# The norms of the first attention's queries and keys: roots and inverses by 32x32 blocks instead of whole tiles

## The chip, the cores and the metric

The kernel runs on one core of a Trainium2 chip. The metric is the device time of one execution in microseconds. A core has a matrix engine (TensorE, PE in the profile), a vector engine (VectorE, DVE), an engine for functions (ScalarE, ACT), a general engine (GpSimd, POOL) and a queue engine (SyncE, SP). Each executes its own instructions in the order in which they are written; semaphores order them against each other.

## The reference, cut to what matters

The model has two blocks on 512 tokens of 1024 features. The change lies in the attention of the first one: 16 query heads and 4 key heads of 64 features, each divided by the root of the mean of its squares, turned by the rotary tables, and then used in softmax attention.

```
q = rms_norm(q.reshape(b, s, N_Q_HEADS, HEAD_DIM), q_norm_w[l])
k = rms_norm(k.reshape(b, s, N_KV_HEADS, HEAD_DIM), k_norm_w[l])
v = v.reshape(b, s, N_KV_HEADS, HEAD_DIM)
q = axial_rope(q, cos_r, sin_r, cos_c, sin_c)
k = axial_rope(k, cos_r, sin_r, cos_c, sin_c)
attn = block_attention(q, k, v)
```

where rms_norm multiplies by `lax.rsqrt(jnp.mean(xf * xf, axis=-1, keepdims=True) + EPS)`.

## The kernel before, in words

Activations lie with features on the 128 partitions and the 512 tokens along them. A feature tile is 128 output features by 512 tokens: 24 matmuls on PE (8 blocks of the input, three products each, since every operand is split into a high and a low part), done by `feature_tile` (L1411), whose argument `mid` puts other PE work into the middle of the tile.

The weights come as one stream of slabs: SP loads them, ACT makes the high part (L775), POOL the low part (L716), and PE uses them. ACT's high parts are written out by `hi_upto` ahead of the tile at hand; POOL's other work (the rotation products L668 and L669 of a tile) stands at given slabs of this stream.

The list `QK` gives the order of the ten tiles of keys and queries: k0, q0, k1, q1, q2 up to q7. A tile holds two heads. After k1 come four value tiles (`value_tiles`, L1710), one for each 128 tokens, 24 half-width matmuls each. Key, query and value tiles use two PSUM banks in turn, so the fourth value tile needs the bank of the second one back.

For one tile the work is:
- ACT, `qk_copy` (L948): squares of the tile into `sq`, and a copy of the tile, with the norm's gain, into `t`; the copy frees the bank.
- DVE, `swap_halves` (L2440): a shuffle that swaps the halves for the rotation; POOL then makes its two products (`rotate`, L661).
- PE, `qk_stat` (L1491), in the middle of the next tile: `blk64` times the squares, into the bank `PST`. Each output row is the mean over the 64 features of its head, so all 64 rows of a head are equal. It waits for the semaphore `qk_std`, that is for the root of the tile before, as there is one `PST`.
- ACT, `qk_root` (L956): the root of 128x512 elements into `std`. It waits for PE's sum and for the inverse of the tile before. In ACT's order it stands ahead of the next tile's `qk_copy`; k1's root stands behind the copy of the first value tile and ahead of that of the second (L985 to L990); q5's stands ahead of the tanh of a gate tile, and q6's ahead of the row of maxima of head 0.
- DVE, `qk_inverse` (L2452): the reciprocal of 128x512 elements into `rstd`; then `rotated` (the add L2449, which waits for both of POOL's products) and the product with `rstd` (`turn_k` L2462, `turn_q` L2481), and for some tiles the split into high and low parts.

The last two tiles, q6 and q7, are inverted and turned inside the attention loop over 16 heads (L2543), their reciprocals in halves (`half_inverse`, L2457). In the same loop DVE takes the maxima of scores (`max_of`, L2520), which PE needs back before it writes the next scores of that kind; the four maxima of head 0 are taken between the shuffle and the inverse of q5 (L2532).

Of the kernel before, what the change touches and what calls it, by code (L numbers as in the profile page):

```python
# [9 lines left out]
ACT = mybir.ActivationFunctionType  # L10
# [3 lines left out]
P = 128  # L14
# [12 lines left out]
NCH = SEQ // P  # L27
# [241 lines left out]
for _name, _w in NORMS:  # L269
# [11 lines left out]
    _s += POOLED.get(_name, 0) == _w  # L281
    SUM_AT[_name] = _s
ADA_W = 2 * D_MODEL
ADA_G = 3
# [53 lines left out]
def build(nc, d):  # L338

    with ExitStack() as ctx:  # L340
# [64 lines left out]
        mx = [maxima[:, 0:NCH], maxima[:, NCH:2 * NCH]]  # L405
        inv_sum = small[:, 312:320]

        with Arena():
# [21 lines left out]
            with Arena():  # L430
# [7 lines left out]
                qF = sb("q_full", [P, QT, SEQ])  # L438
                std_last = sq_sum
            with Arena():  # L440
# [141 lines left out]
        chunks_added, sums_taken, sums_inverted, inverse_turned = exp_masked, st_done, rec_done, xt_done  # L582
        inverse_kept, q_high, inverse_spread = x_kept, e_ready, xs_sc
        ADDED_AT, SCANNED = 2 * PAIRS, PAIRS

        def token_half(half):
# [168 lines left out]
        def _(act):  # L755
# [200 lines left out]
            def qk_root(name):  # L956
                act.wait_ge(stat_mm, SUM_AT[name])
                if name == QK[-1]:
                    out = std_last
                else:  # L960
                    out = std
                    if QK_AT[name]:
                        act.wait_ge(qk_inv, QK_AT[name])
                A(out[:, :], PST[:, :], ACT.Sqrt, bias=eps).then_inc(qk_std, 1)

# [414 lines left out]
        def _(pe):  # L1380
# [110 lines left out]
            def qk_stat(name):  # L1491
                n = STAT_AT[name][0]
                pe.wait_ge(sq_ready, n + 1)
                if QK_AT[name]:
                    pe.wait_ge(qk_std, QK_AT[name])
                else:
                    pe.wait_ge(rows_kept, 1)
                mm(PST[:, :], blk64, sq[n % 2][:, :], start=True, stop=True).then_inc(stat_mm, 1)
# [262 lines left out]
            def take_sums(u, hh):  # L1761
# [3 lines left out]
                else:  # L1765
                    pe.wait_ge(qk_std, len(QK))
                for i in range(NCH):
# [358 lines left out]
        def _(ve):  # L2126
# [319 lines left out]
            def rotated(name):  # L2446
# [3 lines left out]
                v.settle()  # L2450

            def qk_inverse(name):  # L2452
                ve.wait_ge(qk_std, QK_AT[name] + 1)
                V.reciprocal(rstd[:, :], std[:, :]).then_inc(qk_inv, 1)  # L2454
                ve.wait_ge(qk_inv, QK_AT[name] + 1)

            def half_inverse(name, half):  # L2457
                ve.wait_ge(qk_std, QK_AT[name] + 1)
                src, w = std_last if name == QK[-1] else std, slice(half * SEQ // 2, (half + 1) * SEQ // 2)
                v(V.reciprocal(rstd[:, w], src[:, w]))  # L2460

            def turn_k(j):  # L2462
                swap_halves(("k", j))
                qk_inverse(("k", j))
                rotated(("k", j))
# [61 lines left out]
            for name in QK[:-2]:  # L2527
# [4 lines left out]
                if name == ("q", QT - 3):  # L2532
                    for i in range(NCH):
                        max_of(0, i)
                qk_inverse(name)
                turn_q(name[1])
# [3 lines left out]
                if name[1] == 1:  # L2540
                    split_q(2)
            swap_halves(QK[-2])
            for h in range(N_Q):  # L2543
                if h + 1 < N_Q:
                    for i in range(NCH):
                        max_of(h + 1, i)
                u = h // 2
                if h in (1, 3):
                    half_inverse(QK[-2], h // 2)
                if h == 5:  # L2550
                    turn_q(QT - 2)
                    swap_halves(QK[-1])
                if h in (7, 9):
                    half_inverse(QK[-1], h // 2 - 3)
                if h == 1:
# [682 lines left out]
```

## Time and profile before

| | |
|---|---|
| median of 3 runs | 1561.52 us (1560.51 to 1563.8) |
| the profiled execution | 1560.5 us, its span 1558.7 us |
| PE busy | 1528.3 us, 98% |
| DVE, ACT, POOL busy | 1139.1, 834.7, 907.3 us |
| granted clock of PE | 0.998 |
| the stage of key, value and query tiles | about 458 to 540 us of the span |
| the attention loop | about 540 to 650 us |

Busy time of an engine is the union of its instructions. Matmul ends are modelled, so for PE the distance from one matmul's start to the next says more than the busy share. Times in the rows are microseconds from the start of the span, and the time of one instruction in nanoseconds where a column says mean ns.

### The profile page before, as it was taken

How to read it: one execution, taken by the hardware profiler on the slowest of the kernel's cores; microseconds unless marked ns; L12 is line 12 of the kernel's file. 1: busy time of each engine (PE TensorE's matmuls, PEld its weight loads, DVE VectorE, ACT ScalarE, POOL GpSimd, SP SyncE). 2: the span in 40 equal slices, each digit the busy share in tenths (PEclk: the TensorE clock that was granted, in tenths of full speed). 3: DMA queues.
4: the chain of work that ended last, by engine and by line, in shares of the span. 5: the costliest groups of instructions: out<-in, count | busy, mean ns of one | idle time of the engine just before them, and what ended most of it. 6: DMA issues, size and time to landing. Idle time of an engine off the chain costs nothing.

```text
span 1558.7 us, 23051 instructions
## 1 busy us (share of the span) xinstructions
PE 1528.3 (98%) x7975; PEld 1235.0 (79%) x7975; DVE 1139.1 (73%) x1590; ACT 834.7 (54%) x1552; POOL 907.3 (58%) x644
## 2 busy tenths in 40 slices
PE   7999999999999999999999999999999999999998
PEld 4778888888878766687777888888888888888887
DVE  4799888888739888488459878877768895567542
ACT  4775765766633587423344444444458665454442
POOL 0556765766655876556846767776753467532314
PEclk9999999999999999999999999999999999999999
DMA  8434434434332300276622333333422334322212
GB/s 328 133 122 129 128 108 130 131 107 129 115 94 70 81 28 1 83 239 249 214 67 83 96 92 103 108 109 109 113 83 81 95 102 122 94 62 69 68 41 82
DMA packets 77485, 171.34 MB, mean 110 GB/s; under 512 B 8321, under 2 KB 10753, under 8 KB 73921
## 3 DMA queue, kind: packets, MB, share of 16 engines
q1 hardware_dynamic: 70064, 133.09, 28.7%
q10 hardware_dynamic: 7312, 36.83, 6.7%
q8 instruction: 65, 1.06, 0.3%
q14 instruction: 44, 0.35, 0.1%
HBM read 167.67 MB, written 2.23 MB: 109 GB/s over the span
## 4 chain that ended last, share of the span: by engine, by line
PE 64%; DVE 13%; issue 8%; POOL 6%; DMA 2%; ACT 2%; ACTq 0%; DVEq 0%; POOLq 0%; SPq 0%
PE bank L1401 8%; PE bank L1403 7%; PE bank L1402 7%; PE bank L1419 7%; PE bank L1422 7%; PE bank L1420 7%; POOL w_lo L716 6%; PE bank L1864 4%; DMA w_raw<-ws 2%; PE bank L1866 2%; DVE ada_acc L2155 2%; PE bank L1757 2%; DVE rstd L2454 2%; PE bank L2021 1%; PE bank L1695 1%
## 5 line engine op out<-in xcount | busy, mean ns | idle before, releaser
L716 POOL TENSOR_TENSOR w_lo<-w_raw,w_hi 128x512 fp32r<-128x512 f32 x440 | 644.8, 1489 | 403.2 <-ACT w_hi L775 402.8
L775 ACT ACTIVATE w_hi<-w_raw 128x512 fp32r<-128x512 f32 x444 | 260.4, 624 | 124.0 <-DMA w_raw<-ws 104.2
L1401 PE MATMUL bank<-a_hi_and_lo,w_hi 128*128 128x512 f32 (+1 forms) x800 | 315.8, 395 | 2.4 <-ACT gates_early L840 1.2
L1403 PE MATMUL bank<-a_hi_and_lo,w_lo 128*128 128x512 f32 (+1 forms) x800 | 308.7, 386 | 0.0
L1402 PE MATMUL bank<-a_hi_and_lo,w_hi 128*128 128x512 f32 (+1 forms) x800 | 308.3, 385 | 0.0
L1419 PE MATMUL bank<-b_hi,w_hi 128*128 128x512 f32 x536 | 210.2, 392 | 2.6 <-ACT tmp L1119 1.4
L1422 PE MATMUL bank<-b_lo,w_hi 128*128 128x512 f32 x536 | 209.2, 390 | 0.0
L1420 PE MATMUL bank<-b_hi,w_lo 128*128 128x512 f32 x536 | 209.0, 390 | 0.0
L1401 PEld LDWEIGHTS bank<-a_hi_and_lo,w_hi 128*128 128x128 f32 x800 | 150.4, 188 | 36.6 <-issue 4.4
L1402 PEld LDWEIGHTS bank<-a_hi_and_lo,w_hi 128*128 128x128 f32 x800 | 150.5, 188 | 30.8 <-issue 1.9
L1403 PEld LDWEIGHTS bank<-a_hi_and_lo,w_lo 128*128 128x128 f32 x800 | 150.3, 188 | 30.8
L1419 PEld LDWEIGHTS bank<-b_hi,w_hi 128*128 128x128 f32 x536 | 100.7, 188 | 24.4 <-ACT tmp L1119 1.8
L1422 PEld LDWEIGHTS bank<-b_lo,w_hi 128*128 128x128 f32 x536 | 100.6, 188 | 21.7 <-DVE b_lo L2694 0.5
L1420 PEld LDWEIGHTS bank<-b_hi,w_lo 128*128 128x128 f32 x536 | 100.7, 188 | 20.4
L647 POOL TENSOR_TENSOR square_sum<-square_sum,sq 128x512 f32<-128x512 f32 x33 | 50.0, 1515 | 60.5 <-ACT sq L787 60.3
L1864 PE MATMUL bank<-input_sums_hi_lo,w_hi 128*128 128x512 f32 x208 | 75.3, 398 | 1.7 <-DVE tmp L2699 1.5
L915 ACT ACTIVATE M<-cs_rows,log_dt_minus_cs 128x128 f32<-128x128 f32 x256 | 76.5, 388 | 0.0
L2268 DVE SCALAR_TENSOR_TENSOR tmp<-bank,small,tmp 128x510 f32<-128x510 f32 (+1 forms) x96 | 71.8, 749 | 4.8 <-ACT tmp L865 1.5
L2381 DVE TENSOR_TENSOR C_decayed<-C_decayed,C_feat 128x2048 f32<-128x2048 f32 x16 | 50.2, 3140 | 17.6 <-ACT C_decayed L906 17.6
L1866 PE MATMUL bank<-input_sums_hi_lo,w_lo 128*128 128x256 f32 x208 | 58.4, 281 | 0.0
L1864 PE MATMUL bank<-a_hi_and_lo,w_hi 128*128 128x512 f32 x156 | 56.1, 393 | 0.0
L2524 DVE TENSOR_REDUCE maxima<-bank 128x1 fp32r<-128x512 f32 x64 | 43.7, 690 | 16.5 <-PE bank L1729 15.8
(447 smaller groups left out, 3183.2 us busy)
## 6 DMA issues: line engine op xcount, KB each, us to landing
w_raw<-ws SPq DMA_DIRECT2D x457, 256.0 KB, 2.7
cs_rows<-cs_scratch ACTq DMA_DIRECT2D x16, 1024.0 KB, 5.2
ada_piece<-ada ACTq DMA_DIRECT2D x16, 1024.0 KB, 5.3
ada_piece<-ada SPq DMA_DIRECT2D x8, 1024.0 KB, 17.6
x_stream<-x SPq DMA_DIRECT2D x2, 1024.0 KB, 8.5
x_stream<-x ACTq DMA_DIRECT2D x1, 2048.0 KB, 7.8
out<-x_stream SPq DMA_DIRECT2D x4, 256.0 KB, 3.3
out<-x_stream SPq DMA_DIRECT2D x8, 128.0 KB, 1.8
```

The source lines that it names most:

```text
L716: nc.gpsimd.tensor_tensor(wlo[b][:, :], full[:, :], r32(whi[b][:, :]), ALU.subtract)\
L775: A(whi[n % RING][:, :], full[:, :], ACT.Copy).then_inc(hi_done, 1)
L915: ins = A(Dm[:, r, w], csB[:, r, w], ACT.Identity, bias=lnCs[:, c, h:h + 1])
L1401: mm(out, lh, rh, start=first, stop=False)
L1402: mm(out, lh, rl, start=False, stop=False)
L1403: return mm(out, ll, rh, start=False, stop=last)
L1419: mm(gb(name)[:, :], whi[b][:, o:o + P], hi(k), start=(k == 0), stop=False)
L1420: mm(gb(name)[:, :], wlo[b][:, o:o + P], hi(k), start=False, stop=False)
L1422: ins = mm(gb(name)[:, :], whi[b][:, o:o + P], lo(k), start=False, stop=(k == blocks - 1))
L1864: mm(out[:, :].rearrange("p (two n) -> p two n", two=2), whi[b][:, o:o + P], both, start=(first and j == 0), stop=False, skip_group_check= ...
L1866: ins = mm(out[:, LEFT], wlo[b][:, o:o + P], both[:, 0, :], start=False, stop=(j == BPS - 1), skip_group_check=True)
L2268: ins = V.scalar_tensor_tensor(out[:, o], src[:, s], cwh[:, j * 24 + i:j * 24 + i + 1], out[:, o], ALU.mult, ALU.add)
```

## The change

The sum of a tile in `PST` is turned in 32x32 blocks by DVE (`qk_to_columns`) into `std`. As all rows of a head are equal, all 32 columns of a turned block are equal, and its 32 rows are the tokens of the block: one column of each of the 16 blocks holds everything. ACT takes the root of these 128x16 elements only, DVE their reciprocal, and a second transpose of DVE, which reads each of the 16 columns 32 times, turns them back into `rstd`. The roots, in two buffers by turns, and the inverses use columns of `cwh`, which earlier stages are done with. A count `qk_columns` (the semaphore `bt_ev`, already at N_GROUPS) tells of the first transpose. ACT's root waits for it instead of PE's sum, PE's next sum waits for it instead of ACT's root. The maxima of head 0 are split: two in the old place, two behind the loop's last tile. The reciprocals in halves in the attention loop become whole ones, q6's at head 1 and q7's at head 7, and q7's first transpose stands behind the first maximum of head 1.

```
-        inv_sum = small[:, 312:320]
+        inv_sum, qk_inverses, qk_roots = small[:, 312:320], cwh[:, 112:128], [cwh[:, 80:96], cwh[:, 96:112]]
...
+        def columns_of(wide):
+            return wide[:, :].rearrange("p (b c) -> p b c", c=SQUARE)
...
             def qk_root(name):
-                act.wait_ge(stat_mm, SUM_AT[name])
-                if name == QK[-1]:
-                    out = std_last
-                else:
-                    out = std
-                    if QK_AT[name]:
-                        act.wait_ge(qk_inv, QK_AT[name])
-                A(out[:, :], PST[:, :], ACT.Sqrt, bias=eps).then_inc(qk_std, 1)
+                j = QK_AT[name]
+                act.wait_ge(qk_columns, N_GROUPS + j + 1)
+                if j >= 2:
+                    act.wait_ge(qk_inv, j - 1)
+                A(qk_roots[j % 2], columns_of(std)[:, :, 0], ACT.Sqrt, bias=eps).then_inc(qk_std, 1)
...
                 if QK_AT[name]:
-                    pe.wait_ge(qk_std, QK_AT[name])
+                    pe.wait_ge(qk_columns, N_GROUPS + QK_AT[name])
...
-                    pe.wait_ge(qk_std, len(QK))
+                    pe.wait_ge(qk_columns, N_GROUPS + len(QK))
...
+            def qk_to_columns(name):
+                j = QK_AT[name]
+                ve.wait_ge(stat_mm, SUM_AT[name])
+                if j:
+                    ve.wait_ge(qk_std, j)
+                V.transpose(std[:, :], PST[:, :]).then_inc(qk_columns, 1)
+
             def qk_inverse(name):
-                ve.wait_ge(qk_std, QK_AT[name] + 1)
-                V.reciprocal(rstd[:, :], std[:, :]).then_inc(qk_inv, 1)
-                ve.wait_ge(qk_inv, QK_AT[name] + 1)
-
-            def half_inverse(name, half):
-                ve.wait_ge(qk_std, QK_AT[name] + 1)
-                src, w = std_last if name == QK[-1] else std, slice(half * SEQ // 2, (half + 1) * SEQ // 2)
-                v(V.reciprocal(rstd[:, w], src[:, w]))
+                j = QK_AT[name]
+                ve.wait_ge(qk_std, j + 1)
+                V.reciprocal(qk_inverses, qk_roots[j % 2]).then_inc(qk_inv, 1)
+                ve.wait_ge(qk_inv, j + 1)
+                v(V.transpose(columns_of(rstd), qk_inverses[:, :, None].broadcast_to([P, SEQ // SQUARE, SQUARE])))
 
             def turn_k(j):
                 swap_halves(("k", j))
+                qk_to_columns(("k", j))
                 qk_inverse(("k", j))
...
                 if name == ("q", QT - 3):
-                    for i in range(NCH):
+                    for i in range(NCH // 2):
                         max_of(0, i)
+                qk_to_columns(name)
                 qk_inverse(name)
...
+            for i in range(NCH // 2, NCH):
+                max_of(0, i)
             swap_halves(QK[-2])
+            qk_to_columns(QK[-2])
             for h in range(N_Q):
                 if h + 1 < N_Q:
                     for i in range(NCH):
                         max_of(h + 1, i)
+                        if h == i == 0:
+                            qk_to_columns(QK[-1])
                 u = h // 2
-                if h in (1, 3):
-                    half_inverse(QK[-2], h // 2)
+                if h == 1:
+                    qk_inverse(QK[-2])
...
-                if h in (7, 9):
-                    half_inverse(QK[-1], h // 2 - 3)
+                if h == 7:
+                    qk_inverse(QK[-1])
```

## Rows read from the trace of the kernel before

**Rows 1.** The page: the span, and each engine's busy time, share and instructions.
```profile
span 1558.7 us, 23051 instructions
...
PE 1528.3 (98%) x7975; PEld 1235.0 (79%) x7975; DVE 1139.1 (73%) x1590; ACT 834.7 (54%) x1552; POOL 907.3 (58%) x644
```
**Rows 2.** Busy time by stretches: length, then each engine's, clock, DMA.
```profile
458.00:484.00 26.00, 26.00 (x158) 22.43 (x157) 21.04 (x26) 10.39 (x20) 12.13 (x10) 1.00 0.19 51
...
520.00:540.00 20.00, 19.16 (x80) 13.93 (x79) 16.64 (x15) 12.52 (x18) 17.07 (x13) 1.00 0.31 88
```
**Rows 3.** Timeline of PE, waits only: start, length, line, operation, [idle before, releaser].
```profile
527.36 1.10 PE L1729 MATMUL bank<-k_hi_over_lo,q_hi_twice 128*128 128x512 f32 x2 [0.45 <-DVE maxima L2524]
...
536.84 1.12 PE L1498 MATMUL bank<-sq,consts 128*128 128x512 f32 x2 [0.19 <-ACT sq L787]
...
580.52 0.50 PE L1729 MATMUL bank<-k_hi_over_lo,q_hi_twice 128*128 128x512 f32 x1 [0.34 <-DVE maxima L2524]
```
**Rows 4.** Groups by line and shape: busy us, mean ns, idle before.
```profile
L2524 DVE TENSOR_REDUCE maxima<-bank 128x1 fp32r<-128x512 f32 x64 | 43.7, 690 | 16.5 <-PE bank L1729 15.8
...
L2444 DVE STREAM_SHUFFLE tmp<-tmp 128x512 f32<-128x512 f32 x10 | 7.4, 744 | 0.1
...
L2508 DVE RECIPROCAL small<-bank 128x8 f32<-128x8 f32 x8 | 1.7, 207 | 4.9 <-PE bank L1768 4.9
...
L791 ACT ACTIVATE roots_by_token<-bank,small 128x4 f32<-128x4 f32 x7 | 1.8, 262 | 5.3 <-PE bank L1470 5.3
```
**Rows 5.** Timeline of DVE, tile q4.
```profile
512.09 0.75 DVE L2444 STREAM_SHUFFLE tmp<-tmp 128x512 f32<-128x512 f32 x1
512.72 3.34 DVE L2454 RECIPROCAL rstd<-std 128x512 f32<-128x512 f32 x1
516.09 1.22 DVE L2449 TENSOR_TENSOR tmp<-tmp 128x512 f32<-128x512 f32 x1
517.34 1.66 DVE L2483 TENSOR_TENSOR q_full<-tmp,rstd 128x512 f32<-128x512 f32 x1
```
**Rows 6.** Timeline of PE: the sums of q3 and q4, one tile apart.
```profile
504.53 1.02 PE L1498 MATMUL bank<-sq,consts 128*128 128x512 f32 x2
...
510.87 1.02 PE L1498 MATMUL bank<-sq,consts 128*128 128x512 f32 x2
```
**Rows 7.** Timeline of DVE: the same cast in k0 and in k1.
```profile
468.92 0.42 DVE L2475 CAST k_hi_over_lo<-tmp 64x512 fp32r<-64x512 f32 x1
...
489.89 1.40 DVE L2475 CAST k_hi_over_lo<-tmp 64x512 fp32r<-64x512 f32 x1
```
**Rows 8.** Timeline of ACT: roots of k0 and k1, copy of the second value tile.
```profile
462.40 0.69 ACT L964 ACTIVATE std<-bank,small 128x512 f32<-128x512 f32 x1 [1.35 <-PE bank L1498]
...
478.10 0.69 ACT L964 ACTIVATE std<-bank,small 128x512 f32<-128x512 f32 x1 [3.34 <-PE bank L1403]
478.69 0.38 ACT L989 ACTIVATE v_by_token<-bank 128x256 f32<-128x256 f32 x1
```
**Rows 9.** Timeline of DVE: inverse and add of k0, q0, and the shuffle of k1.
```profile
463.12 3.35 DVE L2454 RECIPROCAL rstd<-std 128x512 f32<-128x512 f32 x1 [2.81 <-ACT std L964]
466.51 0.69 DVE L2449 TENSOR_TENSOR tmp<-tmp 128x512 f32<-128x512 f32 x1
...
472.69 0.77 DVE L2444 STREAM_SHUFFLE tmp<-tmp 128x512 f32<-128x512 f32 x1
...
476.71 1.21 DVE L2449 TENSOR_TENSOR tmp<-tmp 128x512 f32<-128x512 f32 x1
...
482.92 0.75 DVE L2444 STREAM_SHUFFLE tmp<-tmp 128x512 f32<-128x512 f32 x1
```
**Rows 10.** Timeline of POOL: the second rotation product of k0 and of q0.
```profile
463.08 1.30 POOL L669 TENSOR_TENSOR tmp<-tmp,rope_table 128x512 f32<-128x512 f32 x1
...
474.83 1.29 POOL L669 TENSOR_TENSOR tmp<-tmp,rope_table 128x512 f32<-128x512 f32 x1
```
**Rows 11.** Timeline of PE: the first matmul of the fourth value tile.
```profile
480.78 0.28 PE L1401 MATMUL bank<-w_hi,a_hi_and_lo 128*128 128x256 f32 x1
```

More of the change, by code:

```diff
@@ L282 @@
     SUM_AT[_name] = _s
+SQUARE = 32
 ADA_W = 2 * D_MODEL
@@ L438, in build @@
                 qF = sb("q_full", [P, QT, SEQ])
-                std_last = sq_sum
             with Arena():
@@ L582, in build @@
         chunks_added, sums_taken, sums_inverted, inverse_turned = exp_masked, st_done, rec_done, xt_done
-        inverse_kept, q_high, inverse_spread = x_kept, e_ready, xs_sc
+        inverse_kept, q_high, inverse_spread, qk_columns = x_kept, e_ready, xs_sc, bt_ev
         ADDED_AT, SCANNED = 2 * PAIRS, PAIRS
+        def columns_of(wide):
+            return wide[:, :].rearrange("p (b c) -> p b c", c=SQUARE)
         def token_half(half):
```

## The prediction
> **What bounds the kernel now.** I read the page's busy line first: TensorE (PE) is busy 1528.3 of 1558.7 us [rows 1]. The reader should see that no other engine is near that, so a change on VectorE (DVE) and ScalarE (ACT) moves the end only where it makes or removes a gap on PE. Next the table by stages: the stage of the change, 458 to 540 us, has PE at 26.00 of 26 us in its first part and 19.16 of 20 us in its last [rows 2]. Then PE's timeline, for its gaps: a matmul on the q tiles waits 0.45 us for DVE's row maxima at 527.36, the last norm's matmul waits 0.19 us for ACT at 536.84, and in the attention loop one waits 0.34 us for maxima at 580.52 [rows 3]. The chain of waits runs through DVE's reciprocals in this stage, which tempts one to count them as time to be won; but a chain is not a gap on PE, and PE has none beside them. Last DVE's timeline: from the shuffle to the end of the product a q tile takes it 6.9 us (512.09 to 517.34 + 1.66 = 519.00), of which 3.34 is the reciprocal, 1.22 the add and 1.66 the product [rows 5]. PE needs 6.34 us a tile (504.53 to 510.87) [rows 6]. So DVE falls behind by 0.6 us a tile, and that lag is what PE meets at 527.36.
>
> **The cost of the new pieces.** No 32x32 transpose is in the trace. Its nearest row is the shuffle of the same 128x512 tile at 0.744 us; the reduction that reads 128x512 from PSUM takes 0.690 [rows 4]. I take T = 0.70 for each transpose. From below 0.42, the cheapest 512-column DVE row (a cast of 64 partitions, next to it the same cast at 1.40 when POOL is at work) [rows 7]; from above 3.34, the reciprocal, the dearest 128x512 row. The root of 16 columns stands between that of 4 columns (0.262) [rows 4] and of 512 (0.69) [rows 8], near the first: 0.27. The reciprocal of 16 columns is near that of 8, 0.207 [rows 4]: 0.20. A hand-over between engines took 0.03 from the end of k0's root (462.40 + 0.69 = 463.09) to its reciprocal (463.12), and 0.04 from there to the add on one engine [rows 8, 9]; I take 0.06 and 0.03.
>
> A tile's norm on DVE was 3.34; it becomes T + 0.06 + 0.27 + 0.06 + 0.20 + 0.03 + T = 2.0. But the add behind it also needs POOL's two rotation products, which start at the end of the shuffle. For q0 the second one ends at 474.83 + 1.29 = 476.12 [rows 10], 3.43 us from the start of the shuffle, against 4.02 until the add before (472.69 to 476.71) [rows 9]. The gain is 0.6 us a tile, not 1.3: POOL is late next. A q tile then takes DVE about 3.43 + 1.22 + 1.66 = 6.3 us, PE's own rate, and the lag no longer grows.
>
> The Trainium skill bears on this, SBUF — State Buffer, section "Who interferes with whom": a DVE instruction with one SBUF input outside the two-port modes doesn't contend with GpSimd, one with two SBUF inputs does. The long reciprocal, with one input, was free cover for POOL's products, and the transposes would be as free; by this T stays 0.70 and the sum below stands. If the transposes met POOL as the cast did (1.40 for 0.42), each back transpose would grow by up to 1 us, partly under the POOL wait, and the sum would be about 1.3 us higher. No row of a transpose decides it.
>
> Vector Engine (DVE) Microarchitecture Reference of the Trainium skill, section 3.8, says that shuffle and transpose use one reorder array and that the transpose sustains one element per cycle per lane. No run shows it yet; by it T would be that of the shuffle.
>
> **The new wait, k1 and the v tiles.** This is the term that I think decides the sign. ACT's root L964 of tile j waited for PE's sum and the inverse of j-1. Now it waits for DVE's transpose of j, and DVE comes to that only after it has finished tile j-1. Behind k1's root ACT has the copy of the second v tile (478.69) [rows 8], whose bank the fourth v tile needs; PE starts that one at 480.78 [rows 11]. So: when is k1's transpose done?
> - k0: sum ready at 462.40. Transpose to 463.1, root 463.4, reciprocal 463.65, back transpose 464.4. POOL's second product ends at 463.08 + 1.30 = 464.38. The add starts at 464.45 instead of 466.51: 2.05 gained, of which I give back 0.2, since POOL's weight work may now fall on the add (1.22 with POOL at work at 516.09, 0.69 without at 466.51) [rows 5, 9].
> - q0: 0.6 gained, as above. Together 2.45.
> - k1: its shuffle starts at 482.92 - 2.45 = 480.5, ends 481.15, transpose 481.9, root from 481.95 to 482.2, v copy 0.39 long [rows 8] to 482.5, PE 482.5 instead of 480.8.
> So PE stands still for 1.7 us where it had no gap. Nothing behind absorbs it: the weights are then further ahead, not less, and the later gaps are waits for other engines that move with PE. If the two hand-overs and the contention go well it is 1.3, if badly 2.3.
>
> **The steady q tiles.** PE's sum of tile j now waits for the transpose of j-1 instead of its root. With DVE's lag shrinking that is done some 4 us before (for q3: swap near 508, sum at 504.53 + 1.7 needs only q2's, at about 502.5). ACT is held by its root until the transpose; it then copies the next tile, whose bank PE wants a whole tile later. Cost 0. Its cover is 4 to 6 us; at T above 1.3 it starts to go.
>
> **Moved maxima.** DVE takes maxima 0 and 1 at about 521.5 instead of 526.63, as its lag is 5 us less. The gap at 527.36 goes, 0.45 and the start behind it, which I put at another 0.15: -0.6. Maxima 2 and 3 come behind q5's product, before 530, and their reader is in the middle of the last tile, after 531: nothing. The root of q6 waits for its sum, then a transpose, then loads its table (1.28), and is done near 535.1 instead of 534.5, but PE is 1.1 later too. The gap at 536.84 shrinks by about 0.15.
>
> **Attention loop.** Two reciprocals of 1.74 us per tile become one of 0.2 and a transpose; three maxima wait behind q7's transpose by 0.7, and q7's root comes 0.7 later but takes 0.4 less. DVE is not what PE waits for, but for the 0.34 at 580.52, which comes from the add and product of q6 ahead of the maxima and stays. 0, with -0.3 to +0.5 as bounds.
>
> **Sum.** +1.7 - 0.6 - 0.15 = +0.95. Of the profiled run's own 1560.5 us that makes 1561.4; the median of the three runs, 1561.5, lies 1.0 above it. Predicted: 1562.4. A difference of 0.2%, 3.1 us, is about what can be told from no change here, so I forecast no change.
>
> **Rivals.**
> 1. Transposes of 4-byte elements are slow, T about 2 us (slower). For: no row of this operation. Against: the shuffle at 0.744. k0's chain would end at 467.0 (+0.5), q0's add 1.2 later than before, so k1's root at 487.6 and the v gap 7.2; each q tile would take DVE 0.65 + 4.6 + 2.9 = 8.1 against PE's 6.34, 1.8 us a tile for the last three or four: 13 in all, 1574. It starts to be slower by 3.1 us at T near 1.3, where the v gap is about 3.7 (five more transposes before the copy, each 0.6 longer, less what POOL's wait covers). Chance 0.09.
> 2. The v gap is larger than worked out, through ACT's queue: k1's square is held behind q0's root until 472.4, and POOL's weight subtractions fall on DVE's adds, products and splits in other places, up to 0.5 to 1 us each (0.69 against 1.22 for one add) [rows 5, 9]. Then +3.5 to +5, some 1565.5. Chance 0.08.
> 3. No v gap, as k0 and q0 gain more than 2.45 us, and DVE's and POOL's earliness takes away all gaps up to 600 us. These are 0.84 in the last part of the stage [rows 2] and about as much in the loop: at most -2 us, 1559.5, still within 0.2%. More than -3.1 would need the weight stream to come earlier in later stages, for which no row speaks. Chance of the no-gap case 0.15, of a time 0.2% faster 0.09.
> 4. The change doesn't do what it says, the sums being spread over 64 partitions so that 16 columns would not hold all: they do, each 32x32 block has equal rows, and a transposed block has equal columns. Chance nil.
>
> My forecast (a v gap of 1 to 2.5 us, the rest about even) has 0.68. Faster is the 0.09 of rival 3, slower rivals 1 and 2, 0.17, and the same the rest, 0.68 + 0.15 - 0.09 = 0.74. The range: 1559.0 takes in rival 3, 1566.5 rival 2; rival 1 is left out, and the sum's own bounds (+0.4 to +2) lie well inside.
>
> **What would show it.** A PE gap of 1 to 2.5 us at 481, released by ACT's v copy, with ACT's root idle before it on DVE's transpose: right. No wait there, or over 3 us: step "k1" wrong. A transpose at 0.65 to 0.80 in each direction; one at 1.3 or more makes T wrong. DVE idle before the add of each q tile with POOL's product as the releaser: POOL is late next. No gap at the third maxima matmul near 528. DVE's shuffle of q5 near 521 instead of 526. If the time falls by over 3 us with PE's gaps unchanged, the whole view that PE's gaps set the end is wrong.

## The result, and the profile after

| | before | changed |
|---|---|---|
| median of 20 runs each, in turn | 1561.05 us (1559.73 to 1565.22) | 1564.94 us (1562.22 to 1567.8) |
| ratio, 95% interval | | 1.0022 (1.0016 to 1.0029) |
| the profiled execution | 1560.5 us, span 1558.7 | 1562.2 us, span 1560.4 |

The changed kernel is slower by 3.9 us by the medians, 3.4 by the ratio (2.5 to 4.5 by its interval). The prediction called a difference of 0.2% or 3.1 us the same; this one is just above that, and clear of zero. The time lies inside the predicted range, 2.5 above the predicted 1562.4. The profiled execution is the fastest of its 20, so its whole span says less than the distances inside the stage; I read those. Ratios are taken over runs in the same state, beside runs of the kernel before made at the same time; one run of experiment 12 took 3622.59 us and is in no ratio.

The page, first lines as in [rows 1]:
```profile
span 1560.4 us, 23070 instructions
...
PE 1528.9 (98%) x7975; PEld 1236.5 (79%) x7975; DVE 1129.1 (72%) x1608; ACT 829.6 (53%) x1552; POOL 907.4 (58%) x644
```
DVE has 10 us less to do, and the time is longer. PE is "busy" 0.6 us more with the same matmuls. The stretches show why (columns as in [rows 2]; the third number from the end is PE's granted clock):
```profile
458.00:484.00 26.00, 22.91 (x132) 19.29 (x131) 20.52 (x32) 8.35 (x19) 14.03 (x11) 1.00 0.18 51
484.00:485.00 1.00, 1.00 (x7) 1.00 (x7) 0.41 (x1) 0.00 (x0) 1.00 (x2) 0.55 0.00 0
485.00:487.00 2.00, 2.00 (x11) 2.00 (x10) 1.97 (x2) 0.00 (x0) 0.80 (x1) 0.50 0.02 6
487.00:488.00 1.00, 1.00 (x8) 0.95 (x7) 0.93 (x4) 0.09 (x1) 0.00 (x0) 0.74 0.84 225
488.00:520.00 32.00, 32.00 (x135) 25.00 (x134) 25.86 (x34) 13.80 (x28) 24.70 (x18) 1.00 0.28 84
...
520.00:540.00 20.00, 20.00 (x87) 15.38 (x86) 13.23 (x17) 9.88 (x16) 16.84 (x13) 1.00 0.27 80
```
PE stands still for 3.1 us before 484, where it had no gap [rows 2]. Then its clock is 0.50, the 1.2 GHz level, for some 3 us. PE counts as busy there, but its matmuls start 0.21 us apart instead of 0.12. The stop and what follows in PE's timeline, as against 480.78 in [rows 11] and the stops in [rows 3]:
```profile
483.24 0.39 PE L1401 MATMUL bank<-w_hi,a_hi_and_lo 128*128 128x256 f32 x1 [3.09 <-ACT v_by_token L989]
...
485.52 0.41 PE L1402 MATMUL bank<-w_lo,a_hi_and_lo 128*128 128x256 f32 x1
...
495.89 1.02 PE L1498 MATMUL bank<-sq,consts 128*128 128x512 f32 x2
...
539.09 1.02 PE L1498 MATMUL bank<-sq,consts 128*128 128x512 f32 x2
...
582.97 0.50 PE L1729 MATMUL bank<-k_hi_over_lo,q_hi_twice 128*128 128x512 f32 x1 [0.34 <-DVE maxima L2529]
```
The stops at 527.36 and 536.84 are gone, the one of 0.34 is there still. To compare positions take both from the sum of k0 (461.34 before, 460.55 after, so 0.8 us come from upstream). The sum of q1 comes 4.8 later (30.51 to 35.34 us behind k0's), of q6 3.8, of q7 3.0 and the attention loop 3.3. So 4.8 is lost at the value tiles: the fourth one starts 3.3 later (22.69 behind k0's sum, 19.44 before), and the slow clock costs the other 1.5 (experiment 2). At the maxima and the last norm 1.8 is gained.

### The profile page after: what moved, and what is told of

Same layout as the page of the kernel before. It is cut to its first block, busy times and chain, and to the rows that moved or that the text cites. A ratio compares the mean times of both kernels' runs of the same rounds, so it can differ in the third digit from the quotient of the medians.

```text
span 1560.4 us, 23070 instructions
## 1 busy us (share of the span) xinstructions
PE 1528.9 (98%) x7975; PEld 1236.5 (79%) x7975; DVE 1129.1 (72%) x1608; ACT 829.6 (53%) x1552; POOL 907.4 (58%) x644
## 3 DMA queue, kind: packets, MB, share of 16 engines
q8 instruction: 65, 1.06, 0.3%
## 4 chain that ended last, share of the span: by engine, by line
PE 72%; DVE 8%; issue 8%; POOL 5%; ACT 1%; DMA 1%; ACTq 0%; POOLq 0%; DVEq 0%; SPq 0%
PE bank L1401 9%; PE bank L1403 9%; PE bank L1402 9%; PE bank L1419 8%; PE bank L1422 8%; PE bank L1420 8%; PE bank L1864 5%; POOL w_lo L719 4%; PE bank L1866 3%; DVE ada_acc L2155 2%; PE bank L1757 1%; PE bank L2021 1%; PE bank L1695 1%; PE bank L1749 1%; DMA w_raw<-ws 1%
```

## The pieces, read from the trace after

Groups by line and shape (busy us, mean ns), for [rows 4] and the 3.35 us inverse of [rows 9]:
```profile
L2464 DVE STREAM_TRANSPOSE rstd<-small 128x512 f32<-128x512 f32 x10 | 7.1, 711 | 0.3
L2457 DVE STREAM_TRANSPOSE std<-bank 128x512 f32<-128x512 f32 x10 | 7.1, 705 | 6.0 <-PE bank L1498 6.0
L2462 DVE RECIPROCAL small<-small 128x16 f32<-128x16 f32 x10 | 2.5, 252 | 3.2 <-ACT small L964 3.2
...
L964 ACT ACTIVATE small<-std,small 128x16 f32<-128x16 f32 x10 | 3.2, 324 | 36.6 <-DVE std L2457 29.0 <-issue 7.5
```
Each piece is within 0.06 us of its estimate. Now DVE's timeline of k0, q0 and k1, for [rows 9]:
```profile
461.61 0.72 DVE L2457 STREAM_TRANSPOSE std<-bank 128x512 f32<-128x512 f32 x1 [2.10 <-PE bank L1498]
...
463.64 1.75 DVE L2449 TENSOR_TENSOR tmp<-tmp 128x512 f32<-128x512 f32 x1
...
466.48 1.50 DVE L2481 CAST k_hi<-tmp 64x512 fp32r<-64x512 f32 x1
...
474.44 1.77 DVE L2449 TENSOR_TENSOR tmp<-tmp 128x512 f32<-128x512 f32 x1 [0.71 <-POOL tmp L672]
...
481.19 0.72 DVE L2444 STREAM_SHUFFLE tmp<-tmp 128x512 f32<-128x512 f32 x1
...
510.07 0.73 DVE L2444 STREAM_SHUFFLE tmp<-tmp 128x512 f32<-128x512 f32 x1
...
513.51 1.78 DVE L2449 TENSOR_TENSOR tmp<-tmp 128x512 f32<-128x512 f32 x1 [0.72 <-POOL tmp L672]
515.32 1.65 DVE L2488 TENSOR_TENSOR q_full<-tmp,rstd 128x512 f32<-128x512 f32 x1
```
k0's add starts 2.1 us earlier against k0's sum, as predicted. But it now starts 0.09 us behind a weight subtraction of POOL, and takes 1.75 instead of 0.69. The q tile in [rows 5], which is q3's and not q4's, shows the same: its add came 0.62 behind the start of a subtraction before and comes 0.07 behind it after, and ends 1.84 and 1.85 behind the subtraction's start, so being earlier wins nothing. POOL's row in the kernel before, beside the add at 516.09 of [rows 5]:
```profile
515.47 2.98 POOL L716 TENSOR_TENSOR w_lo<-w_raw,w_hi 128x512 fp32r<-128x512 f32 x2
```
POOL's rows in the changed kernel:
```profile
463.55 1.29 POOL L719 TENSOR_TENSOR w_lo<-w_raw,w_hi 128x512 fp32r<-128x512 f32 x1
...
512.17 1.30 POOL L672 TENSOR_TENSOR tmp<-tmp,rope_table 128x512 f32<-128x512 f32 x1
513.44 2.98 POOL L719 TENSOR_TENSOR w_lo<-w_raw,w_hi 128x512 fp32r<-128x512 f32 x2
```
The Trainium skill (SBUF — State Buffer, section "Who interferes with whom") says that two inputs in SBUF, or a cast in a two-port mode, make a DVE instruction wait for all of a GpSimd instruction begun before it. The trace agrees: add 1.75 to 1.78 and cast 1.50 beside POOL, and the transposes, with one input, 0.69 to 0.72 whether POOL works or not. In which mode the cast runs the trace doesn't say.

## The experiments

Theories after the comparison: the loss is the new wait (ACT's root behind DVE's order), its size set by contention with POOL, and the clock adds to it. The rivals: the new operations cost it, or the slow clock came from elsewhere. Ratios are to the kernel before, with 95% intervals, from 5 to 12 runs beside 15 to 35 of the kernel before; they need not equal the quotient of the medians.

**1. The wait taken off the value tiles.** In the changed kernel, k1's root goes behind the copy of the third value tile.
```
                         tile_in(("v", c))
-                        if c == 1:
-                            qk_root(name)
                         inc_evac(A(vv[:, c, :, :], ...
+                        if c == 2:
+                            qk_root(name)
```


> The changed kernel with one thing moved: ScalarE takes k1's root behind the copy of the third value tile instead of ahead of the copy of the second. Theory (the loss is the stop of TensorE ahead of the fourth value tile, 3.1 us idle and then 3.4 us at half the granted clock, together 4.8 us): the gap near 481 goes, the granted clock stays 1.00 in 484 to 520 us, and the time is 4.5 to 5 us under the changed kernel's 1564.9, about 1560.2, some 1 us under the kernel before. Rival 1 (the loss lies in later waits of the attention loop): the gap goes and the time stays near 1564. Rival 2 (the gap only moves, to the first q tile, as ScalarE is held at the root all the same): a gap of 1 us or more at the start of q1, time 1562 to 1563.


Measured 1562.05 us, 1.0007 (0.9998 to 1.0016). The stop at 483 is gone, the clock is 1.00 from 484 to 520. So the wait makes stop and slow clock, and the new operations alone don't. But the time is 1.9 above my 1560.2, where rival 2 put it, and PE's timeline has two new stops, at the sums of q3 and q4 and not at q1:
```profile
507.34 1.13 PE L1498 MATMUL bank<-sq,consts 128*128 128x512 f32 x2 [1.74 <-ACT sq L790]
514.22 1.12 PE L1498 MATMUL bank<-sq,consts 128*128 128x512 f32 x2 [0.29 <-ACT sq L790]
```
These squares stand on ACT behind the root of the tile before, which waits for DVE's transpose: that root starts at 506.49, the squares at 506.71, PE at 507.34. The 4.8 us lost earlier had hidden that wait.

**2. PE kept at work in the stop.** The changed kernel, with 18 bf16 matmuls of constants in front of the fourth value tile (their result is not used).
```
+                    if c == NCH - 1:
+                        for _ in range(18):
+                            mm(bank[7][:, 0:3 * P], identb, cstb[:, :], start=True, stop=True)
                     start(("v", c))
```


> The changed kernel with 18 small bf16 matmuls of 384 columns into an unused bank ahead of the fourth value tile's wait; about 0.16 us each, 2.9 us, so that TensorE works through the stop instead of idling. The stop itself stays: the fourth value tile still starts at about 483.2. Theory (part of the loss is the clock, which is granted at half speed after the idle stretch): the clock stays 1.00 after it, and the time falls by 1.7 us from the changed kernel's, to 1563.2. Rival (the clock's fall is not tied to this stop, or is in the idle time already): no change, 1564.9, and the rows after the stop still show 0.50.


Measured 1562.72 us, 1.0008 (1.0000 to 1.0017). PE's timeline:
```profile
479.79 3.10 PE L1715 MATMUL bank<-consts_bf 128*128 128x384 bf16 x18
483.04 0.39 PE L1401 MATMUL bank<-w_hi,a_hi_and_lo 128*128 128x256 f32 x1 [0.16 <-ACT v_by_token L989]
```
The real work starts as late as in the changed kernel, but the clock stays 1.00, and the fourth value tile takes 2.98 us instead of 4.48; the sum of q1 is 33.86 us behind k0's, 1.5 less than in the changed kernel. That is the clock's part in this stage. In the time it is 2.2 by the two ratios, which were measured apart and are not sharp enough to tell 2.2 from 1.5.

**3. k1 ahead of the splits.** The changed kernel, but DVE turns k1's halves and blocks before it splits the queries of q0.
```
             def turn_k(j):
-                swap_halves(("k", j))
-                qk_to_columns(("k", j))
+                if j == 0:
+                    swap_halves(("k", j))
+                    qk_to_columns(("k", j))
...
                 if name[1] == 0:
+                    swap_halves(("k", 1))
+                    qk_to_columns(("k", 1))
                     split_q(0)
                     split_q(1)
```


> The changed kernel with VectorE's shuffle and first transpose of k1 moved ahead of the two splits of q0 into high and low parts (3.15 us from 477.94 to 481.1). Theory (the gap is as long as VectorE is late for k1's transpose): the gap shrinks from 3.1 us by 3.0 to 3.2 to 0 to 0.2 us and the clock stays up: 1560.2 to 1560.5. Rival (ScalarE's own queue makes it late): the gap stays over 1 us, 1562 or more.


Measured 1561.49 us, 1.0001 (0.9993 to 1.0010). The stop at the value tile is gone without touching ACT, as expected. The time is 1.0 to 1.3 above what I expected, as PE stops at 505.74 (1.00 us) and 512.65 (0.30), where it did in experiment 1. What costs is where DVE's order puts the transpose, not the transpose.

**4. Less of POOL's work.** The changed kernel with four of POOL's weight subtractions, between the shuffles of k0 and k1, cut to 32 of 512 columns (it leaves out the low parts of the other columns).
```
-                nc.gpsimd.tensor_tensor(wlo[b][:, :], full[:, :], r32(whi[b][:, :]), ALU.subtract)
+                short = slab_of(("k", 0)) + 8
+                w = slice(0, 32) if isinstance(n, int) and short <= n < short + 4 else slice(0, SLAB)
+                nc.gpsimd.tensor_tensor(wlo[b][:, w], full[:, w], r32(whi[b][:, w]), ALU.subtract)
```


> The changed kernel with the four subtractions of GpSimd on weight slabs that run between k0's and k1's shuffles cut from 512 columns to 32 (the low parts of these slabs are left out for the rest). Theory (the gap came out as 3.1 instead of 1.7 us because VectorE's adds and casts wait for GpSimd: the adds of k0 and q0 took 1.75 and 1.77, a cast 1.50, a product 1.66): these take 0.69, 0.69, 0.42 and 0.69, k1's transpose comes 4 us earlier, the gap is gone, time 1560 to 1560.5. Rival (the adds are slow of themselves behind a transpose): they stay at 1.7, the gap at 3.1 us, time 1564 to 1565.


Measured 1559.72 us, 0.9991 (0.9982 to 1.0000). DVE's timeline:
```profile
465.40 0.71 DVE L2451 TENSOR_TENSOR tmp<-tmp 128x512 f32<-128x512 f32 x1
...
474.08 0.73 DVE L2451 TENSOR_TENSOR tmp<-tmp 128x512 f32<-128x512 f32 x1 [0.72 <-POOL tmp L672]
...
478.83 0.75 DVE L2446 STREAM_SHUFFLE tmp<-tmp 128x512 f32<-128x512 f32 x1
```
From k0's transpose to k1's shuffle it is 15.46 us; in the changed kernel 19.58. So contention with POOL takes 4.1 us there. In the kernel before it took about 2.4 (a product 1.65 and one 1.67 for 0.69, an add 1.21 for 0.69), so the change moved DVE's work into 1.7 us more of it, where the prediction gave back 0.2. PE has no stop up to 545. From q2 on, where POOL's work is whole again, DVE's shuffles are 6.94 apart as in the changed kernel (501.08, 508.02, 514.97).

This experiment also tells what becomes of the loss. Its sum of q7 is 73.71 us behind k0's, 1.8 less than before and 4.83 less than in the changed kernel (78.54), and the attention loop keeps the whole 4.83. So the 1.8 gained is the change's own, and nothing of the 4.8 is made up for.

**5. The lag removed by ACT's order?** Experiment 1, and from q2 on ACT squares and copies a tile ahead of the root of the one before.
```
-                if late_root:
+                if late_root and n <= KVT:
                     qk_root(QK[n - 1])
                 qk_copy(name)
+                if late_root and n > KVT:
+                    qk_root(QK[n - 1])
```


> The changed kernel with k1's root behind the copy of the third value tile, and, from q2 on, ScalarE's squares and copy of a tile ahead of the root of the tile before. With the root of k1 moved alone, TensorE stood 1.74 and 0.29 us at the sums of q3 and q4, waiting for squares that stood behind the root of the tile before, 2.0 in all. Theory (the new wait of the root for VectorE's transpose holds up everything behind it on ScalarE): both stops go, nothing comes in their place up to 545 us, and the time is 2 us under that kernel's 1562.05: 1559.7 to 1560.3, 0.05 to 0.1% under the kernel before. Rival (VectorE is late anyway, so that TensorE meets its lag at the next point, the maxima behind q5 or the sum of q6): a stop of 1 to 2 us near 527 or 532, time 1561.5 to 1562.


Measured 1562.35 us, 1.0012 (1.0003 to 1.0021): my expectation missed, its rival came. PE's timeline:
```profile
506.70 1.10 PE L1501 MATMUL bank<-sq,consts 128*128 128x512 f32 x2 [0.96 <-DVE std L2460]
513.64 1.10 PE L1501 MATMUL bank<-sq,consts 128*128 128x512 f32 x2 [0.38 <-DVE std L2460]
530.88 0.50 PE L1404 MATMUL bank<-a_hi_and_lo,w_hi 128*128 128x512 f32 x1 [0.57 <-ACT gates_early L843]
```
With ACT out of the way PE waits for DVE itself, which is still 6.92 us a tile.

**6. The reciprocal made short in the kernel before.** Its width is 16 columns instead of 512 for q0, k1 and q1 to q5 (it leaves out the norms of the other columns).
```
-                V.reciprocal(rstd[:, :], std[:, :]).then_inc(qk_inv, 1)
+                w = slice(0, 16 if QK_AT[name] else SEQ)
+                V.reciprocal(rstd[:, w], std[:, w]).then_inc(qk_inv, 1)
```


> The kernel before, with the reciprocals of q0 to q5 and k1 cut from 512 columns to 16 (the other columns of the inverse are left as k0's, so the norms are left out there). The chain as before, without transposes, so VectorE has 3.1 us a tile less to do. In the changed kernel a q tile takes VectorE 6.92 us from shuffle to shuffle, as before (6.95). Theory (the pace is set by GpSimd: two products behind the shuffle, then a weight subtraction for which VectorE's add waits): the period stays 6.9 us, with VectorE idle before the add; the gaps of TensorE at 527 and 537 shrink by the 1 us or so that VectorE gains once in the q0 and k1 tiles, time 1560 to 1561.5. Rival (the reciprocal sets the pace in the kernel before, the transposes' round trip over ScalarE in the changed one): the period falls to 5.5 us or less, or to TensorE's 6.34, and the gaps go altogether: 1559.5.


Measured 1562.19 us, 1.0003 (0.9994 to 1.0012). DVE's timeline:
```profile
507.52 0.72 DVE L2444 STREAM_SHUFFLE tmp<-tmp 128x512 f32<-128x512 f32 x1
508.14 0.23 DVE L2455 RECIPROCAL rstd<-std 128x16 f32<-128x16 f32 x1
511.02 1.69 DVE L2449 TENSOR_TENSOR tmp<-tmp 128x512 f32<-128x512 f32 x1 [2.66 <-POOL tmp L669]
...
514.44 0.75 DVE L2444 STREAM_SHUFFLE tmp<-tmp 128x512 f32<-128x512 f32 x1
```
3.1 us of a tile's work are gone and a tile takes 6.9 us as before: DVE waits 2.66 for POOL's products, then behind POOL's weight subtraction. In the DVE time of a steady tile the change could win nothing; that work was hidden. The time came out a little above the 1560 to 1561.5 that I expected. PE's stop at the maxima is still there (0.42); the one before q7's sum is gone, and that sum is 0.6 earlier.

**7 and 8. A delay put into the kernel before.** Behind k1's root ACT makes 8, or 5, copies of a spare tile one after the other (0.63 us each), which hold the value copy.
```
                             qk_root(name)
+                            for _ in range(8):
+                                a(A(t[4][:, :], t[5][:, :], ACT.Copy))
+                                a.settle()
```


> The kernel before with eight copies of 0.63 us on ScalarE, one after the other, ahead of the copy of the second value tile: 5.0 us, of which 1.7 is slack, so that TensorE stops for 3.3 us before the fourth value tile, with nothing else changed. Theory (a stop of this length also costs a stretch of some 3.4 us at the granted clock 0.50, that is 1.7 us, and a later TensorE then meets less of VectorE's lag, which gives back 1.0 to 1.8): granted clock 0.50 in the table of stages behind the stop, the first q tile 5.0 us later than before, the gaps at 527 and 537 gone, time 3.2 to 4 us over before. Rival 1 (the fall of the clock in the changed kernel comes from something else): clock 1.00, first q tile 3.3 us later, time +1.5 to +2.3. Rival 2 (nothing is given back): +5.0.

> The same with five copies, 3.15 us, so a stop of 1.4 us. It asks whether the clock falls after a stop of this length as well. If it does: granted clock 0.50 for some stretch behind it, the first q tile 3 us later. If it doesn't: 1.00, the first q tile 1.4 us later, and with up to 1.4 us given back at the gaps of 527 and 537 the time is within 0.5 us of before.


Measured 1564.29 us with 8 (1.0027, 1.0016 to 1.0038) and 1562.91 with 5 (1.0012, 1.0002 to 1.0021). With 8, PE's first matmul behind the stop, and the stretch behind it:
```profile
483.37 0.58 PE L1404 MATMUL bank<-w_hi,a_hi_and_lo 128*128 128x256 f32 x1 [3.47 <-ACT v_by_token L992]
```
```profile
484.00:486.00 2.00, 2.00 (x11) 2.00 (x11) 1.97 (x2) 0.00 (x0) 2.00 (x3) 0.50 0.00 0
```
The same two with 5:
```profile
486.00 0.39 PE L1404 MATMUL bank<-w_hi,a_hi_and_lo 128*128 128x256 f32 x1 [1.49 <-ACT v_by_token L992]
```
```profile
486.00:488.00 2.00, 2.00 (x16) 2.00 (x17) 1.96 (x4) 0.23 (x1) 0.61 (x1) 1.00 0.00 0
```
A stop of 3.47 takes the clock with it, q1's sum is 5.0 late, 4.3 of that arrives at the attention loop (the stop at the maxima is gone, the one of 0.19 before q7's sum is not), and the time is 4.2 longer by the ratio (2.5 to 5.9). A stop of 1.49 leaves the clock at 1.00 and costs 1.7 at q1, 1.0 at the loop and 1.9 in the time (0.3 to 3.3), where I had expected to be within 0.5. So a stop at this place brings the slow clock with it and is enough for a loss of the changed kernel's size, with no new operation in the kernel.

**9. The kernel before with the new wait alone.** ACT's root waits for DVE's shuffle of its tile; no operation is changed.
```
                 act.wait_ge(stat_mm, SUM_AT[name])
+                if name != QK[-1]:
+                    act.wait_ge(swapped, QK_AT[name] + 1)
```


> The kernel before, its arithmetic untouched, with the changed kernel's new dependency alone: ScalarE takes a tile's roots only when VectorE has turned the halves of that tile (which stands behind VectorE's work for the tile before). Theory (the loss is in that dependency and in no operation): VectorE's turn of k1 ends at 483.6 (by the time of the kernel before), ScalarE's root is over at 484.3, the copy of the second value tile behind it at 484.7; TensorE stands still 3.3 to 4.0 us there, its clock falls to half for some 3 us, the sum of q1 comes 4.8 to 5.6 us late, time 1564.3 to 1565.8. Rival (the loss is in the transposes and the small roots): as the kernel before, 1561.0 to 1561.6.


Measured 1570.36 us, 1.0061 (1.0047 to 1.0075): more than I expected, and far from the rival. ACT's timeline, then PE's:
```profile
484.67 0.69 ACT L966 ACTIVATE std<-bank,small 128x512 f32<-128x512 f32 x1 [7.46 <-DVE tmp L2446]
```
```profile
485.68 0.58 PE L1403 MATMUL bank<-w_hi,a_hi_and_lo 128*128 128x256 f32 x1 [3.44 <-ACT v_by_token L991]
...
544.43 0.47 PE L1751 MATMUL bank<-q_hi_twice,k_hi_over_lo 128*128 128x512 f32 x1 [2.67 <-issue]
```
The clock is 0.50 from 486 to 490 here, and q1's sum comes 7.1 late. The row of 2.67 names no releaser, but ACT's timeline shows what ended it:
```profile
541.74 1.28 ACT L966 ACT_TABLE_LOAD   x1 [5.89 <-DVE tmp L2446]
...
543.75 0.58 ACT L970 ACTIVATE q_lo<-bank 1x512 fp32r<-1x512 f32 x1
```
It is the new wait again: q6's root waits for DVE's shuffle, head 0's row of maxima stands behind that root, and PE's first scores with this row start 0.10 behind its end (0.09 in the kernel before). The clock is 0.50 from 547 to 549 once more. So the wait alone is enough for the loss, and the rest of the change makes it smaller: 9.5 us by the ratio against 3.4.

**10 and 11. POOL made to wait for the add.** The 6.94 us come from a lock: POOL's products wait for DVE's shuffle, DVE's add waits for the products and then behind POOL's next subtraction. So POOL waits until the add is done. Once in experiment 1's kernel (10), once in the kernel before (11).
```
                 nc.gpsimd.tensor_tensor(t[2]..., rope1[:, 1, :], ALU.mult).then_inc(rot_step, 1)
+                if name in QK[:-2]:
+                    pool.wait_ge(rot_added, j + 1)
...
-                v(V.tensor_tensor(t[3][:, :], t[3][:, :], t[2][:, :], ALU.add))
-                v.settle()
+                V.tensor_tensor(t[3][:, :], t[3][:, :], t[2][:, :], ALU.add).then_inc(rot_added, 1)
+                ve.wait_ge(rot_added, QK_AT[name] + 1)
```


> The changed kernel with the third norm's root behind the copy of the third value tile, and with one new wait: after its two products for a tile, GpSimd starts no low part of a weight before VectorE's sum of those products is done. Theory (GpSimd and VectorE hold each other up; this lock sets 6.94 us a tile, not the norms): VectorE's sum takes 0.7 instead of 1.75, its distance from tile to tile falls from 6.94 to TensorE's 6.34, the stops of TensorE of 1.74 and 0.29 us in front of the sums of the fourth and fifth query tile are gone, and so is the wait for the value tile; time 1559.5 to 1560.5, some 1.5 below the kernel with the root moved alone (1562.05) and at or below the kernel before (1561.0 to 1561.6). Rival (the norm's chain through three engines sets the distance): still 6.9 us a tile, same stops, 1562. Second rival: low parts 0.7 us later make TensorE wait for weights; a stop with the low weights as its releaser, 1562 to 1563.

> The kernel before with that wait alone. Theory: VectorE's sum takes 0.7 instead of 1.2, the reciprocal of 3.33 stays on VectorE, so its distance from tile to tile is 0.63+3.35+0.72+1.67 = 6.4 us instead of 6.95; the stops at 529.8 (0.42) and 536.8 (0.15) are gone, the rest was hidden; time 0 to 0.6 below the kernel before, 1560.5 to 1561.6. If the kernel above is faster than this one by more than 0.5 us, the shorter norms are worth something once the lock is gone; if they are level, nothing. Rival (later low parts make TensorE wait): 1562 or more.


Measured 1560.79 us (1.0000, 0.9991 to 1.0009) for 10 and 1567.38 (1.0043, 1.0029 to 1.0057) for 11. In 10 the adds take 0.69 and DVE's shuffles are 6.35 apart (510.93, 517.28, 523.63), PE's rate; the lock is as described. But of experiment 1's two stops one is gone and the other is 1.38 instead of 1.74, and the time is level with the kernel before, not the 1559.5 to 1560.5 that I expected:
```profile
508.30 1.13 PE L1501 MATMUL bank<-sq,consts 128*128 128x512 f32 x2 [1.38 <-ACT sq L793]
```
DVE's timeline in 11, then PE's:
```profile
488.09 0.69 DVE L2452 TENSOR_TENSOR tmp<-tmp 128x512 f32<-128x512 f32 x1
```
```profile
490.77 0.47 PE L1404 MATMUL bank<-a_hi_and_lo,w_hi 128*128 128x512 f32 x1 [1.88 <-POOL w_lo L719]
```
With the 3.35 us reciprocal the add comes late, POOL with it, and PE waits for weights, 5.0 us in two stops (1.88 and 3.15), each with the clock at 0.50 behind it. Against my expectation of a small gain, the rival came. With the short norm POOL's wait is affordable: 6.6 us lie between 10 and 11, which also differ in the places of k1's root and of the maxima.

**12. The last stop taken away.** Experiment 10, and DVE turns q2's halves and blocks ahead of the last split.
```
                 if name[1] == 1:
+                    swap_halves(("q", 2))
+                    qk_to_columns(("q", 2))
                     split_q(2)
```


> The kernel with the third norm's root behind the third value tile's copy and GpSimd's wait for the sum, and with one more move: VectorE turns the halves of the third query tile and its 32x32 blocks ahead of the last split of a query head (3.5 us there), not behind it. Theory (the stop of 1.38 us left in front of the sum of the fourth query tile is ScalarE's root of the tile before, held back by that split): the turn ends at 504.0 instead of 507.4, the stop is gone, TensorE's sums from q1 on are 6.34 us apart, and the two stops of the kernel before at 527 and 537 stay away; relative to the first sum the sum of q7 comes 1.8 us earlier than before; time 1558.8 to 1559.8, some 1.0 to 1.8 below the kernel before (1560.5 to 1561.6). Rival (GpSimd's products now fall beside the split, its low parts come later and TensorE waits for weights): a stop with the low weights as its releaser, 1561 or more. Second rival (what follows gives it back, as before): no stop up to 545, but the time as the kernel before.


Measured 1559.3 us beside 1561.86 of the kernel before: 0.9988 (0.9979 to 0.9997), as expected. The stretches, with 0.09 us of idle PE in 61:
```profile
484.00:520.00 36.00, 36.00 (x161) 28.62 (x161) 30.10 (x44) 14.18 (x28) 27.96 (x20) 1.00 0.24 69
520.00:545.00 25.00, 24.91 (x109) 19.02 (x108) 12.44 (x22) 14.17 (x23) 20.80 (x16) 1.00 0.34 102
```
The sum of q7 is 73.71 us behind k0's, against 75.50 before: 1.8 gained, and 1.5 of it is left at the loop. It is faster than the kernel before, by 0.12% only, and the interval nearly reaches 1. All its sums from k0's to q7's stand within 0.01 us of where experiment 4 has them, with the lock still closed there: the 1.8 needs PE without stops at the value tiles and at the sums of q3 and q4, not a shorter tile on DVE.

## Why the prediction was right or wrong

**Right: mechanism, place and sign of the main term.** The view that only gaps on PE count held, and so did the gap at the fourth value tile behind ACT's root behind DVE's transpose. T is 0.70, root and reciprocal are as priced, POOL is late next, the maxima's stop is gone, and the attention loop costs 0.3, inside its bounds. Rival 1 fell with T.

**Too small: the size of that term.** The prediction named a stop over 3 us as the sign that its step "k1" is wrong, and the stop is 3.09. The sum's own bounds (+0.4 to +2) don't hold the measured 3.4. The time is inside the range only because that was widened to 1566.5 for rival 2, which had a chance of 0.08; the measured 1564.9 is nearer to that rival's 1565.5 than to the forecast. That the total stayed near "the same" is in part luck.

**Mis-sized: "k1", 1.7 us, measured 4.8.** Two parts.
- "2.05 gained, of which I give back 0.2", with q0's 0.6 "Together 2.45": DVE's shuffle of k1 came only 0.94 earlier (482.92 to 481.19, less the 0.79 of upstream). Against k0's sum 2.1 was won at its add. Beside POOL 1.06 of it was lost at that add and 1.09 at a cast, and 0.97 won at a product (0.68 instead of 1.65). At q0 0.6 was won as worked out, and 0.56 lost at its add. That sums to 0.96. The fourth value tile starts 3.3 later: the 1.7, and the 1.5 not gained. This is the second half of rival 2, POOL's subtractions on DVE's operations; experiment 4 shows it.
- The clock: no term of mine. Behind the stop of 3.1 us came half-speed work that cost 1.5 (experiment 2; experiment 7 shows that a stop here is enough). Whether it would have come behind the 1.7 us that I forecast is not shown: the clock stayed 1.00 behind stops of 1.49 and 1.74 (experiments 8 and 1), but was 0.50 behind one of 1.88 (experiment 11).

**Right: "Nothing behind absorbs it".** Between experiment 4 and the changed kernel 4.83 us lie at q1, at q7 and at the loop, and by the two ratios 4.8 in the time.

**Mis-sized: the maxima, -0.6, measured -1.07, and the last norm, -0.15, measured -0.72.** The step from q5's to q6's sum went from 13.34 to 12.27. It is 12.26 also in experiments 7 and 9, where the maxima are not split but PE is late, and in experiment 4, where they are split and PE is not late. So either cause is enough, and the gain is that of the whole distance between the sums, not of the 0.45 stop that is marked. The reason given, DVE at q5's shuffle near 521, was wrong: it comes at 523.95. The last norm's gain belongs to the short norms: it is 0.72 in experiment 4 and 0.63 in experiment 6, while in 7 and 8, with the long ones and PE late, this step grows by 0.36 and 0.35.

**Wrong: "a q tile then takes DVE about 3.43 + 1.22 + 1.66 = 6.3 us, PE's own rate".** It takes 6.94 (510.07 to 517.01), as before. I found that POOL's products come last, yet added the old 1.22 for the add behind them. An add that starts 0.07 us behind POOL's subtraction takes 1.78, so both kernels need 5.22 us from the shuffle to the end of the add. Experiment 6 shows that the reciprocal was hidden whole.

**Wrong: "Cost 0" for the steady tiles.** I asked when PE wants the bank of ACT's next copy, and left out that its next sum wants the squares, which ACT makes just ahead of that copy and behind the root. It was true only while PE was 4.8 us late. Without the value stop PE stands 1.3 to 2.0 us there in experiments 1, 3 and 5, and q5's sum comes 1.8 to 2.5 later than before.

**Sum.** 3.3 + 1.5 - 1.1 - 0.7 + 0.3 (attention) = 3.3, where the prediction had 0.95. The ratio has 3.4, the medians 3.9.

## What to carry to other kernels

When an operation is moved from one engine's queue to another's, price the new wait by everything queued ahead of it there, and then look at what stands behind the waiting instruction: here 0.3 us of root held a value copy and TensorE. Moving a two-input VectorE operation earlier can put it behind a GpSimd operation and lose what it won; lay both timelines side by side at the new position. A stop on TensorE of some microseconds has to be priced with the clock behind it. And before an operation is shortened, look for what it runs beside: here the reciprocal was hidden behind GpSimd's products, and opening the lock between the two engines shortened VectorE's tile and left the time at that of the kernel before (experiment 10). The 0.12% came when TensorE's own stops were gone (experiment 12).

## What the runs showed of the hardware

- The granted clock was 0.50 behind stops of PE of 3.09 us (the changed kernel), 3.47 (experiment 7), 3.44 and 2.67 (experiment 9), and 1.88 and 3.15 (experiment 11). It stayed 1.00 behind stops of 1.38 (experiment 10), 1.49 (experiment 8) and 1.74 (experiment 1). Matmuls of constants in the stop kept it at 1.00 (experiment 2). The price in this stage was 1.5 to 3 us beside the stop.
- The 128x512 add took 0.69 alone, 1.19 to 1.23 begun some 0.6 us behind the start of a subtraction of POOL, and 1.75 to 1.78 begun 0.07 to 0.09 behind it. The 64x512 cast took 0.42 alone and 1.40 or 1.50 beside one. The transposes took 0.69 to 0.72 in all cases.
- In the kernel before the reciprocal of q3 (512.72, 3.34 long, one input) and POOL's two products (1.29 and 1.30) ran side by side, all at their usual length.
